# A second place for one tile's h at the head of the second gate sweep

## The reference

```python
h = rms_norm(x, norm1_g) * (1 + scale1) + shift1
u, v_a, q, k, v_b, gates = jnp.split(h @ w_in, PROJ_SPLITS, axis=-1)
...
g_a, g_b = jnp.split(g, N_BRANCH, axis=-1)            # g = sigmoid(gates)
merged = g_a * (out_a @ w_pa) + g_b * (out_b @ w_pb)
x = x + gate1 * (merged @ w_o)
h2 = (rms_norm(x, norm2_g) * (1 + scale2) + shift2).reshape(n * l, d)
idx, wts = hier_route(h2, w_rg, b_rg, w_re, b_re)
y = routed_experts(h2, idx, wts, w_gate, w_up, w_down).reshape(n, l, d)
x = x + gate2 * y
```

## Time and profile before

| | |
|---|---|
| median of 3 runs | 1897.4 us (1896.96 to 1900.05) |
| the profiled execution's own time | 1899.67 us |
| its span, first to last instruction | 1898.0 us |
| mean granted TensorE clock | 0.981 of full |
| PE busy | 1830.8 us, 96% |
| DVE, ACT, POOL busy | 60%, 38%, 12% |
| DMA moved | 384.40 MB, 203 GB/s in the mean |

### The profile page before, as it was taken

How to read it: one execution, slowest core, us unless ns; L and a number is a source line. 1 busy time by engine, 2 the same in 40 slices (tenths; PEclk the granted TensorE clock), 3 DMA queues, 4 the chain that set the end, 5 groups by cost and what they waited for, 6 DMA issues and landing times.

```text
span 1898.0 us, 29695 instructions
## 1 busy us (share of the span) xinstructions
PE 1830.8 (96%) x9077; PEld 1381.1 (73%) x9078; DVE 1137.9 (60%) x2171; ACT 727.8 (38%) x1356; POOL 229.4 (12%) x331
## 2 busy tenths in 40 slices
PE   5999999999999999999899999999899999999987
PEld 2787778777567777777588888888477777777632
DVE  3788888888540000001655555556778888888648
ACT  3444444434330000002321221221477777777522
POOL 0100000000000000000101111101322222222111
PEclk7999999999899999999999999999999999999998
DMA  9322212222485444455844344444889869999587
GB/s 373 108 95 112 108 70 106 112 97 91 181 271 192 177 177 177 177 188 185 307 161 151 133 155 144 155 147 166 273 281 354 292 213 337 328 355 313 193 334 316
DMA packets 175851, 384.40 MB, mean 203 GB/s; under 512 B 30184, under 2 KB 104056, under 8 KB 168572
## 3 DMA queue, kind: packets, MB, share of 16 engines
q1 hardware_dynamic: 139836, 321.28, 47.8%
q0 software_dynamic: 19744, 53.89, 7.6%
q10 hardware_dynamic: 16224, 8.65, 1.5%
HBM read 296.80 MB, written 103.73 MB: 211 GB/s over the span
## 4 chain that ended last, share of the span: by engine, by line
PE 66%; DVE 3%; DMA 2%; issue 1%; ACT 1%; ACTq 0%; POOL 0%; DVEq 0%; SPq 0%; POOLq 0%
PE bank L168 18%; PE bank L170 17%; PE bank L169 17%; PE bank L2865 4%; PE bank L2830 2%; PE bank L2008 2%; PE bank L2970 1%; DMA mixer_parts<-oT_split 1%; PE bank L1307 1%; PE bank L2068 1%; DVE late_x L2807 1%; PE bank L2853 1%; DVE expert_down L2802 0%; DMA gathered<-weighted_rows 0%; DMA expert_down<-weighted_rows 0%
## 5 line engine op out<-in xcount | busy, mean ns | idle before, releaser
L168 PE MATMUL bank<-w_mix_hi,hT_hi 128*128 128x512 f32 (+3 forms) x544 | 203.2, 374 | 3.8 <-DVE hT_lo L610 2.5
L1216 DVE SCALAR_TENSOR_TENSOR ma_rows<-tanh_rows,bank 128x512 f32<-128x512 f32 x32 | 20.6, 684 | 310.2 <-PE bank L170 159.9
L2728 DVE TENSOR_TENSOR gate_up_lo<-expert_gate_up,gate_up_hi 128x2048 fp32r<-128x2048 f32 x86 | 196.4, 2288 | 10.9 <-ACT gate_up_hi L2588 9.9
L169 PE MATMUL bank<-w_mix_hi,hT_lo 128*128 128x512 f32 (+3 forms) x544 | 198.8, 365 | 0.0
L170 PE MATMUL bank<-w_mix_lo,hT_hi 128*128 128x512 f32 (+3 forms) x544 | 198.3, 365 | 0.0
L2588 ACT CAST gate_up_hi<-expert_gate_up 128x2048 fp32r (+1 forms) x86 | 165.1, 1923 | 69.0 <-issue 67.2
L168 PE MATMUL bank<-gate_up_hi,gathered_T_hi 128*128 128x512 f32 x352 | 142.5, 405 | 4.9 <-DVE gathered_T_lo L2719 2.1
L170 PE MATMUL bank<-gate_up_lo,gathered_T_hi 128*128 128x512 f32 x352 | 138.4, 393 | 0.0
L169 PE MATMUL bank<-gate_up_hi,gathered_T_lo 128*128 128x512 f32 x352 | 137.9, 392 | 0.0
L168 PEld LDWEIGHTS bank<-w_mix_hi,hT_hi 128*128 128x128 f32 (+1 forms) x544 | 100.6, 185 | 37.0 <-issue 20.3
L170 PEld LDWEIGHTS bank<-w_mix_lo,hT_hi 128*128 128x128 f32 (+1 forms) x544 | 100.6, 185 | 19.1
(11 more groups left out here) (463 smaller groups left out, 3833.9 us busy)
## 6 DMA issues: line engine op xcount, KB each, us to landing
expert_gate_up<-in_w_gate SPq DMA_DIRECT2D x33, 1024.0 KB, 9.6
expert_gate_up<-in_w_up SPq DMA_DIRECT2D x33, 1024.0 KB, 13.1
expert_down<-in_w_down SPq DMA_DIRECT2D x32, 1024.0 KB, 12.7
h_parts<-hT_split SPq DMA_DIRECT2D x16, 1024.0 KB, 5.1
mixer_parts<-oT_split SPq DMA_DIRECT2D x32, 512.0 KB, 8.2
w_ada_part<-in_w_ada SPq DMA_DIRECT2D x16, 1024.0 KB, 10.7
h_parts_b<-hT_split SPq DMA_DIRECT2D x16, 1024.0 KB, 4.9
expert_down<-weighted_rows SPq DMA_DIRECT2D x12, 1024.0 KB, 8.2
```

Source lines behind the costliest of these rows:

```text
L168: nc_mm(out, left[0], right[0], start=first, stop=False)
L169: nc_mm(out, left[1], right[0], start=False, stop=False)
L1216: last = nc.vector.scalar_tensor_tensor(out=ma[:, par, at], in0=tg[:, at], scalar=1.0, in1=ps[2 + n][:, :], op0=ALU.add, op1=ALU.mult)
L2728: nc.vector.tensor_tensor(wg[par][1][:, at], ring[:, bass.ds(slot * GU + n * HG, HG)], wg[par][0][:, at].bitcast(F32), ALU.subtract).then_ ...
```

## The change

`second_h` is a place of 128 x 2048 elements that is taken and given back at once, so that it has the addresses of the two buffers declared behind it, `attn_out` (xo) and `h2_b`, which the sweep first writes later. Tile 2's h goes there. It is asked after the stores of the sweep before, and ahead of the twelve small loads; its wait for `gated` is gone. Tile 3's h is then the next into `hb`, asked behind the twelve small loads and the landing of tile 2's. POOL's wait in front of its three large DMAs goes from two h loads to three. Tile 0's `residual`, which writes `attn_out`, waits for `gated` 3, the end of tile 2's gate product. The first pass of SP's loop is written out, without its h load; the loop starts at 2.

```diff
         h2T = sb("h2_T", [P, D])
+        with nc.sbuf_tensor("second_h", [P, 2 * D], F32R) as second_h:
+            pass
         xo = sb("attn_out", [P, D])
...
-            def load_h(i, first=False):
-                if not first:
-                    sp.wait_ge(gated, i)
+            def load_h(i, place=hb):
                 src = s["hT"][bass.ds(i - 1, 1), :, :].rearrange("o p c -> p (o c)")
-                sp.dma_start(hb[:, :].bitcast(F32), src).then_inc(h_in, 16)
+                sp.dma_start(place[:, :].bitcast(F32), src).then_inc(h_in, 16)
...
-            load_h(1, True)
+            load_h(1)
...
-            load_h(2)
             sp.wait_ge(shared["stored_ma"][0], 16 * (NT // 2 + 1))
             sp.wait_ge(shared["stored_pb"][0], 16 * (NT // 2 + 1))
+            sp.wait_ge(h_in, 16)
+            load_h(2, second_h)
             for n, part in enumerate((GATE1, SCALE2, SHIFT2)):
                 for j in range(4):
                     cols = slice(part * D + j * Q, part * D + (j + 1) * Q)
                     sp.dma_start(mods_s[j * MS:(j + 1) * MS, n, :],
                                  s["ada"][1:1 + DEC_B, cols].unsqueeze(1).to_broadcast([DEC_B, DEC_T, Q])).then_inc(const_in, 16)
+            sp.wait_ge(h_in, 32)
+            sp.wait_ge(gated, 2)
+            load_h(3)
             load_m(2)
             sp.wait_ge(filled, 48)
             stores(0, MS)
             load_x(1)
-            with sp.Fori(1, NT - 1) as i:
+            load_m(3)
+            stores(1)
+            load_x(2)
+            with sp.Fori(2, NT - 1) as i:
+                sp.wait_ge(gated, i + 2)
                 load_h(i + 2)
...
-            pool.wait_ge(h_in, 32)
+            pool.wait_ge(h_in, 48)
...
                 if m == MS:
                     dve.wait_ge(raw_used, 2 * KW)
+                    dve.wait_ge(gated, 3)
...
+            second_left = lambda h, k: second_h[:, (h * KD + k) * P:(h * KD + k + 1) * P]
...
-                product(0, h_left, 0).then_inc(gated, 1)
+                left = second_left if isinstance(i, int) and i == 2 else h_left
+                product(0, left, 0).then_inc(gated, 1)
```

## The result

The changed kernel takes 1902.89 us (median of 18 runs, 1899.47 to 1907.31), the kernel before 1898.55 (18 runs). The ratio is 1.0025, 95% interval 1.0017 to 1.0033: slower by 4.7 us, between 3.2 and 6.3. The forecast was +6.8, in a range that holds the measured time.

What follows compares the result with a forecast made beforehand. PE, busy in 96% of the span, was taken to bound the kernel, losing time only when standing or at the lower clock. Terms 0 + 4.8 + 2.0 + 0 = +6.8 us gave a median of 1904.2, range 1899.5 to 1907.0.

Steps and rivals of the forecast that it cites:

- h(2) asked earlier: Tile 2's h, asked some 4.3 us earlier behind the same loads, lands no sooner: 0, bounds -4.3 to +0.5.
- POOL behind a third load: POOL's fills wait for h(3), asked only after h(2) lands, so out(1) starts later: +4.8 us, bounds +3.3 to +6.5.
- the fills' own time: From POOL's issue of three DMAs to the last landing: 10.7 us taken, against 11.05 before, bounds 9.5 to 11.05.
- F: The moment POOL's fills have landed and the scalar engine casts; out(1) starts 2.50 us after; forecast 4.8 us later.
- The clock: PE's granted clock falls to the lower level behind the new hole and slows out(1): +2.0 us, bounds 0 and 2.2.
- The late residual: DVE's first residual, waiting for tile 2's gate product, is done 1.9 us before the fills land: 0.
- The sum: The parts added over the kernel: 0 + 4.8 + 2.0 + 0 = +6.8 us, median 1904.2.
- rival 1: h(2) asked earlier lands earlier, at 925.2, yet the fills still hold the end: +2.4, 1899.8; chance 0.17.
- (2): Tile 2's gate product alone, not the fills' landing, sets out(1)'s start: -5.6, 1891.8; chance 0.05.
- Rival 3: Fills alone are quicker, landing 3.3 later, and the clock doesn't fall: +3.3, 1900.7; chance 0.05.
- Rival 4: Loads collide: h(2) 0.5 later, h(3) takes 6.4, fills 11.05, clock +2.2: +9.2, 1906.6; chance 0.05.

Runs made afterwards that it cites:

- after_spin: Changed kernel plus 14 products of 128x512 on PE, results thrown away, in the hole between tile 2's gate product and the L2047 matmuls; 1901.42 us.
- before_late_residual: Kernel before with one line of the change: tile 0's residual on DVE waits for tile 2's gate product; 1899.41 us.
- after_copy_apart: Changed kernel, the 1536 KB copy into the h2 rows on its own semaphore; ACT, SP and POOL wait for the two table fills; 1899.68 us.
- place_of_xo: Kernel before with sample loads first, mod_b last, copy on its own semaphore, plus tile 2's h and the first residual's wait as in the change; 1893.29 us.

## Why the prediction was right, and where its sizes were off

*h(2) asked earlier is worth nothing.* Right: the first hole is 5.27 for 5.26, the landing time 14.9, where 14 to 15 was given. That the holes agree to the hundredth is luck: in the other runs that keep this order they go from 4.93 to 5.32. The request came sooner and the backlog ahead of it was the same. The Trainium skill's DMA: Bandwidth & Descriptors, section "Queues, rings and completion order", says that an engine takes a ring's descriptors in order; this trace agrees: 4.3 us sooner asked, 4.4 us longer on the way (14.9 - 10.5).

*POOL behind a third load.* The mechanism held: h(3) asked at T + 5.20, when h(2) was in; landing 4.85, where 5.0 was taken; POOL at T + 10.63, where 10.86 was taken. The step that was mis-sized is the fills' own time: 10.7 taken, in bounds of 9.5 to 11.05; it measured 9.10. I had seen that ma and pb rows shared the DMA engines with the fills before, and gave 0.35 us for being rid of them; it is 1.95 in this pair of profiles. How large the term is in general stays open: after_spin has the change's DMAs and took 10.23, before_late_residual has those of before and took 10.45 for 11.05. So F moved by 2.93 in the change's profile, not 4.8, and by 4.19 in after_spin's.

*The clock.* It fell behind the new hole, as forecast, and cost 1.44 where 2.0 was taken: out(1) had the lower clock for 3 us (944.56 to 947.6), where the gate product before had it for about 4.6. The hole itself was 4.41 us (940.15 to 944.56), not the 5.4 of the forecast. The run with the added products shows that it is the clock. Its size varies: in the other runs in which it fell, the frame is 15.23 to 16.52, 1.6 to 2.9 over the 13.6 without a fall.

*The late residual costs nothing here*: it was done 0.9 us before the cast (941.17, cast at 942.06). The cover was half of the 1.9 that I counted on. Bare, it is 1.15 from T, 1.59 from the product's end.

*The sum.* 2.93 + 1.44 = 4.37 in the profile, against 4.8 + 2.0; the runs give 4.7, between 3.2 and 6.3. The forecast time, 1904.2, is nearer to the measured 1902.89 than the terms deserve: it starts from three runs of before (1897.4), 1.15 below the median of the 18. One reading is wrong, without weight in the sum: 943.14 is the end of the two small L2047 matmuls, and tile 2's gate product ended at 942.99 (its last row is 942.60 + 0.39).

The rivals: that an early request lands early (1) fell with the first hole unchanged; that F doesn't hold out(1) (2) fell with the copy taken out of F; and the run with mod_b behind h gave rival 1 its early landing and still ended later than the change, as F would have it. Rival 3 had the fills nearly right (+3.3), but the clock did fall. Rival 4 fell with h(3)'s 4.85 for 6.4 and the fills' 9.10 for 11.05.

## What to carry to other kernels

Here a request made 4.3 us sooner behind the same loads landed at the same moment, and moving three of these loads made it land 4.0 us sooner: look at what stands ahead of a request, and move that. When a hole on the busiest engine ends with an unnamed releaser, follow the waits of the engines that feed its next step, for two paths can end within a microsecond of each other and closing the nearer hole alone gives nothing, or costs. When a buffer is added, look for counting waits elsewhere that must go up with it: the new count may hang a far chain on a later load.

## What the runs showed of the hardware that was not expected

The time that POOL's three fill DMAs need went with SP's traffic more than I thought: 9.10 us in the change (10.23 in after_spin), where SP's last large loads were asked 4.6 us ahead of them (928.39, POOL at 932.96); 11.05 before (10.45 in before_late_residual), where 1 MB was asked from 1.8 us ahead; 13.08 with 2 MB asked from 0.6 us ahead (926.90, POOL at 927.47). Two profiles of one arrangement differ by 0.6 to 1.1 us, so the profiles give the order of the three and not the size of the steps; what each of SP's loads adds by itself wasn't measured.

The length of PE's hole doesn't by itself say whether the clock falls. In after_copy_apart and in place_of_xo PE stood for the same 1.61 us ahead of the small matmuls (the first row of each pair below, PE's timeline). In the first, the frame behind ran at 1.00; in the second, the clock was at 0.51 from 939.2 on, after six more matmuls at the upper level (the second row of each pair, busy time by stage).

```profile
941.86 0.38 PE L2060 MATMUL bank<-rms_b,quarters 128*128 128x1 f32 x2 [1.61 <-ACT h_b L1683]
942.57:956.21 13.64, 13.18 (x76) 10.71 (x76) 5.67 (x7) 1.50 (x5) 0.75 (x2) 1.00 0.41 136
```

```profile
937.09 0.38 PE L2065 MATMUL bank<-rms_b,quarters 128*128 128x1 f32 x2 [1.61 <-ACT h_b L1684]
939.20:942.60 3.40, 3.40 (x9) 2.65 (x9) 2.79 (x4) 0.00 (x0) 0.00 (x0) 0.51 0.91 199
```

Why it fell in the one and not in the other stays open; each is one profile.
